# A decoder step on one core: sequence 0's keys moved beside the output projection, and the sampled rows' weight stream taken two tiles a visit

## The reference

```python
def project(x, w_in, b_f):           # q, k, v (8 heads of 64), log-sigmoid gate, u (512)
    h = einsum('bsd,dc->bsc', x, w_in)
def fox_prompt(q, k, v, logf):       # causal attention with bias F[q] - F[k], F = cumsum(logf)
def fox_sample(q, k_new, v_new, logf_new, cache_k, cache_v, cache_logf, page_table):
    k_past = cache_k[page_table]     # 32 pages of 128 positions for each sequence
    s = einsum(q, k_all) * HEAD_DIM ** -0.5 + (Fh[..., P:, None] - Fh[..., None, :])
    out = einsum(softmax(s), v_all)
def pool_mix(u_ext, ...):            # windowed means of u (2, 4, 8, 16), a 128x128 product a group
def finish(x, attn, pool, ...):
    mix = concat(attn, pool) @ w_o                         # 1024x1024
    x1 = layer_norm(ALPHA * x + mix, ln1_g, ln1_b)
    ffn = (silu(x1 @ w_gate) * (x1 @ w_up)) @ w_down       # 1024x2816, 1024x2816, 2816x1024
    return layer_norm(ALPHA * x1 + ffn, ln2_g, ln2_b)
```

## Time and profile before

| | |
|---|---|
| median of 3 runs | 1407.01 us (1405.28 to 1410.99) |
| profiled execution | 1407.72 us, span 1405.9, granted clock 0.988 |
| TensorE busy | 1350.8 us (96%), 7605 matmuls |
| VectorE, ScalarE, GpSimd busy | 693.1 (49%), 360.3 (26%), 548.9 (39%) |
| DMA | 255.56 MB, mean 182 GB/s |

### The profile page before, as it was taken

One profiled execution on the slowest core, in us unless ns is written; L12 is line 12 of the kernel. 1 busy time (PEld: TensorE's weight loads), 2 busy tenths in 40 slices (PEclk: granted clock), 3 DMA queues, 4 the chain that ended last, 5 costly groups with the idle time before them and its releaser, 6 DMA issues.

```text
span 1405.9 us, 21277 instructions
## 1 busy us (share of the span) xinstructions
PE 1350.8 (96%) x7605; PEld 1077.6 (77%) x7605; DVE 693.1 (49%) x1033; ACT 360.3 (26%) x527; POOL 548.9 (39%) x260
## 2 busy tenths in 40 slices
...
GB/s 267 95 128 136 150 162 121 151 57 38 60 109 182 92 65 228 268 239 250 221 253 225 279 245 227 245 237 264 202 271 172 182 113 183 214 265 235 230 92 120
DMA packets 111626, 255.56 MB, mean 182 GB/s; under 512 B 12832, under 2 KB 22945, under 8 KB 106136
## 3 DMA queue, kind: packets, MB, share of 16 engines
...
...
## 4 chain that ended last, share of the span: by engine, by line
PE 86%; DVE 6%; issue 2%; ACT 2%; DMA 2%; POOL 1%; SPq 1%; ACTq 0%; DVEq 0%
PE PSM L1422 32%; PE PSM L1440 16%; PE PSM L1180 10%; PE PSM L1370 6%; PE PSM L1246 4%; PE PSM L1462 4%; PE PSM L1193 3%; PE PSM L1232 3%; PE PSM L1507 2%; PE PSM L1401 1%; PE PSM L1520 1%; DMA WR<-xT 1%; PE PSM L1262 1%; DMA WR<-w_in 1%; DVE ACC L1992 1%
## 5 line engine op out<-in xcount | busy, mean ns | idle before, releaser
L815 POOL TENSOR_TENSOR WL<-WR,WH 128x1024 fp32r<-128x1024 f32 x55 | 131.9, 2399 | 431.9 <-ACT WH L1034 431.9
L755 POOL TENSOR_TENSOR AR<-AR,QB 128x1024 f32<-128x1024 f32 x96 | 231.5, 2428 | 104.2 <-DMA AR<-cache_k 90.1
L1422 PE MATMUL PSM<-XH,WH 128*128 128x512 f32 x672 | 216.8, 404 | 0.0
L1422 PE MATMUL PSM<-XH,WL 128*128 128x512 f32 x672 | 210.7, 395 | 0.0
L1422 PE MATMUL PSM<-XL,WH 128*128 128x512 f32 x672 | 210.7, 395 | 0.0
L1963 DVE TENSOR_TENSOR ACC<-ACC,PSM 128x512 f32<-128x512 f32 x160 | 108.7, 683 | 157.6 <-PE PSM L1440 157.4
L1422 PEld LDWEIGHTS PSM<-XH,WH 128*128 128x128 f32 x672 | 121.2, 188 | 62.1 <-issue 37.3
L1034 ACT CAST WH<-WR 128x1024 fp32r<-128x1024 f32 x55 | 57.5, 1047 | 366.3 <-PE PSM L1422 193.5
L1440 PE MATMUL PSM<-R 128*128 128x512 f32 x528 | 150.8, 394 | 0.0
L1422 PEld LDWEIGHTS PSM<-XH,WL 128*128 128x128 f32 x672 | 126.3, 188 | 29.9
L1422 PEld LDWEIGHTS PSM<-XL,WH 128*128 128x128 f32 x672 | 126.2, 188 | 29.6
...
## 6 DMA issues: line engine op xcount, KB each, us to landing
AR<-cache_v SPq DMA_DIRECT2D x256, 256.0 KB, 3.4
AR<-cache_k SPq DMA_DIRECT2D x192, 256.0 KB, 3.5
AR<-ws SPq DMA_DIRECT2D x37, 1024.0 KB, 4.9
...
ACC<-cache_k SPq DMA_DIRECT2D x32, 256.0 KB, 2.9
WR<-cache_k SPq DMA_DIRECT2D x32, 256.0 KB, 3.1
WR<-w_o SPq DMA_DIRECT2D x5, 1024.0 KB, 5.0
```

Of the source, the lines that this page charges most:

```text
L755: pool.tensor_tensor(keys, keys, QB[:].rearrange("p (o n) -> p o n", o=1).to_broadcast([P, KP, AW]), ALU.mult).then_inc(k_mul, 1)
L815: pool.tensor_tensor(lo, WR[:, raw_weight(e), :], hi.bitcast(F32), ALU.subtract).then_inc(ffn_lo, 1)
L1422: ins = pe.matmul(out[:, hc], (hi, lo)[a][:, k * P:(k + 1) * P], x[b][:, k, hc], start=(k == 0 and n == 0), stop=(k == KC - 1 and n == 2))
```

## The change

1. `sample_queries`, the early pieces, their ring, their DRAM scores and the waits for them are removed. The rows' query part is stored from SN to q_d by GpSimd, beside k_s and v_s.
2. Sequence 0's 16 pieces are multiplied by GpSimd ahead of the FFN's first two rests, and reduced by VectorE behind outputs 8 to 22 (KRED0). SP loads them between the weights of the output projection.
3. The FFN loop has 112 pieces: sequence 1's at units 2 to 37 (2.33 apart), the rest at 38 to 334 (3.08 apart). `queries` is gone; QB is loaded in place with a wait for k_mul.
4. The stream's tiles share units in pairs: SUNIT is 402, 402, 406, 406, 422, 422 and so on to 499, 499, 504, 37 tiles in 19 visits; SUMS move from 431, 444, 459, 473, 488, 498 to 428, 441, 456, 471, 486, 496.
5. The ring of the raw w_in tiles has three slots throughout, and tiles that shared SC, PR and PDN have places of their own or others.

```diff
+KRED0 = {8: (0,), 9: (1, 2), 10: (3,)} | {n: (n - 7,) for n in range(11, 23)}
-LATE = NB * NKP - EARLY
-KMUL = tuple(2 + ((NB - 1) * WIN - 18) * n // (LATE - 1) for n in range(LATE))
+LATE = (NB - 1) * NKP
+KMUL = tuple(2 + 35 * n // (NKP - 1) for n in range(NKP))
+KMUL += tuple(38 + ((NB - 2) * WIN - 4) * n // (LATE - NKP) for n in range(1, LATE - NKP + 1))
 KRED = tuple(u + 3 for u in KMUL)
-Q_LOAD = tuple(KMUL[NKP * n + NKP - 1] + 1 for n in range(NB - NE))
+Q_LOAD = tuple(KMUL[NKP * n + NKP - 1] + 1 for n in range(NB - 1))
-ESLOTS = [x for x in range(8, 48) if x % STEPS not in (0, 1, 11, 12, 13)]
-EMUL = tuple(ESLOTS[n * len(ESLOTS) // EARLY] for n in range(EARLY))
-ERED = tuple(x + 1 for x in EMUL)
...
-    units = {step: TSTART + SPAN_S * n // (len(order) - 1) + 3 * (n >= parts("GU", 0)) for n, step in enumerate(order)}
+    units = {step: TSTART + SPAN_S * (n // 2) // (len(order) // 2) + 3 * (n >= parts("GU", 0)) for n, step in enumerate(order)}
...
-SUNIT = {("W", n, 0): MIX + 2 * n for n in range(4)} | STEPS_S
+SUNIT = {("W", n, 0): MIX + 4 * (n // 2) for n in range(4)} | STEPS_S
...
             sp.wait_ge(ob_full, O["pv", SLOTS - 1] + 1)
+            keys(0)
+            keys(1)
             output_load_raw(2)
...
-            queries(NE)
+            sp.dma_start(QB[:], q_d[0:1, :].to_broadcast([P, AW])).then_inc(qb_ld, 16)
             sp.wait_ge(lnew_done, 1)
+            keys(2)
             output_load_raw(3)
...
+            for n in range(3, 6):
+                keys(n)
             output_load_raw(4)
-            for n in range(KS):
-                keys(n)
             sp.wait_ge(misc_st, 16 * 4)
             weight_tile(0)
+            for n in range(6, 11):
+                keys(n)
             sp.wait_ge(o_free, HRT * OC)
             pages(0, VR, 0, t["cache_v"], v_ld)
             pages(1, VR, 1, t["cache_v"], v_ld)
+            for n in range(11, NKP):
+                keys(n)
+            sp.wait_ge(k_mul, NKP)
+            sp.dma_start(QB[:], q_d[1:2, :].to_broadcast([P, AW])).then_inc(qb_ld, 16)
+            for n in range(NKP, NKP + KS):
+                keys(n)
             sp.wait_ge(wo_lo, OC + 1)
             weight_tile(1)
             weight_tile(2)
...
+            for n in range(NKP):
+                multiply(n)
             for e in range(2):
                 rest(e)
...
-            def sample_queries(m):
-                ...
-                if x in (3, 5):
-                    sample_queries((x - 3) // 2)
...
                 if n - 1 in TURN:
                     rows_lo(TURN[n - 1])
+                for c in KRED0.get(n, ()):
+                    reduce_keys(c)
                 if n == OINDEX[RT - 1, 3]:
                     output_lo(4)
```

More of the change, by code:

```diff
@@ L51 @@
 KS = 3
-KE = 4
-NE = 2
-EARLY = NE * NKP
 POOL_PAGES = 320
@@ L489, in entry @@
                 if e >= WS:
-                    before = max(n for n in range(e) if raw_slot(n) == raw_slot(e))
-                    sp.wait_ge(ent_lo, before + 1)
+                    sp.wait_ge(ent_lo, e - WS + 1)
                 if e == 1 or e > KC:
@@ L694, in _ @@
                         pages(n, VR, n % 2, t["cache_v"], v_ld, v_used, n - 1)
-                for n in range(NE + 1, NB):
-                    if u == Q_LOAD[n - NE - 1]:
-                        queries(n)
-                if o == SUBTRACT + 2 and b + 1 < NE:
-                    sp.wait_ge(m_sub, 2 * b + 2)
-                    sp.dma_start(sc, SC_d[b + 1]).then_inc(sc_ld, 16)
+                for n in range(2, NB):
+                    if u == Q_LOAD[n - 2]:
+                        sp.wait_ge(k_mul, n * NKP)
+                        sp.dma_start(QB[:], q_d[n:n + 1, :].to_broadcast([P, AW])).then_inc(qb_ld, 16)
                 if o == G_LOAD and b + 2 < NB:
@@ L724, in _ @@
             link = Chain(pool, pool_chain)
-            for tile, value in ((ones, 1.0), (PN, 0.0)):
+            for tile, value in ((ones, 1.0), (PN, 0.0), (PND, 0.0), (PD, 1.0)):
                 pool.memset(tile[:], value).then_inc(consts, 1)
@@ L777, in _ @@
                         entry_rest(n)
-                for n in range(EARLY):
-                    if EMUL[n] == x:
-                        multiply(n)
             pool.wait_ge(kn_st, 16 * PAIRS)
@@ L1704, in _ @@
                     key_lo(p, 1, 1)
-                for n in range(EARLY):
-                    if ERED[n] == x and EMUL.index(EMUL[n]) == n:
-                        reduce_keys(n)
-                if x in (3, 5):
-                    m = (x - 3) // 2
-                    dve.wait_ge(ob_full, O["q", m] + 1)
-                    dve.tensor_copy(QB[0:NB, 2 * m * P:(2 * m + 2) * P], OB[0:NB, 0:2 * P]).then_inc(ob_free, 1)
                 if x == 2:
```

207 lines of the change are left out of this document (55 added, 152 removed).

## The result

The changed kernel takes 1466.16 us in the median of six runs (1457.45 to 1470.70), the kernel before 1409.61 (1405.28 to 1411.91): a ratio of 1.0405, 95% interval 1.0378 to 1.0432. It is slower by 57 us where 7 were forecast, and far outside the range. The profiled execution took 1457.45 with a span of 1455.7; it was the fastest of the six, 8.7 under their median.

What follows compares the result with a forecast made beforehand. TensorE, busy 96 per cent of the span, was taken as the bound. Terms -7.2 - 1 + 17 + 2 + 4 + 1 - 8.7 = +7.1 gave 1414.8 against the profiled execution, 1414.1 against the median; forecast 1414.5, range 1401 to 1424.

Steps and rivals of the forecast that it cites:

- Attention loop, -8.2: Attention loop: two query products leave TensorE's chain, -7.2 us, and fewer multiplies and reduces there, -1.
- Output projection, +17 and +2 of clock: Output projection: late piece 11 and VectorE's reduces delay TensorE, +17 us (+10 to +19); half clock after the wait, +2.
- three such meetings are 2 of the 17, at that row's size: Output projection: VectorE slowed beside a multiplying GpSimd, 0.74 us lost in the row L1804, three times.
- near +22: Output projection: the term if each meeting cost up to a full multiply, as estimated from the skill page.
- Loop head, +4: FFN loop, units 0 to 44: more pieces loaded by SP ahead of two value chunks, +4 us (0 to +10).
- the forecast's 3 to 8: FFN loop's first window: sign that TensorE's waits for cache_v would sum to 3 to 8 us.
- Rest of the loop, +1: FFN loop behind its head: pieces 3.08 units apart for 3.50, value chunks mostly inside their margin, +1 us (-2 to +5).
- The QB load, nothing: FFN loop: the QB load waits for k_mul but stands one unit behind that multiply, no cost.
- Stream, -8.7: Tail, stream of sampled rows: 18 merged pairs -6.6 us, a stall missed at unit 472 -3.0, a sum at 441 +0.9.
- Rival C: FFN loop: SP saturates, second chunks of V pairs late, +20 us where the forecast had +5, 1429.8; chance 0.13.
- cache_v waits recur in every window: FFN loop: the sign by which the rival that SP saturates would hold.
- Rivals A and B: Output projection: A, reduces hidden, stall 3, 1398.8, chance 0.17; B, only VectorE's own work counts, stall 11, 1407.8, chance 0.20.

Runs made afterwards that it cites:

- skip_as_before: The changed kernel without sequence 1's 16 pieces, the other 96 at the units they had in the kernel before: ratio 1.0078 to the kernel before.
- values_by_act: The changed kernel with the FFN loop's value loads, page reads too, on ScalarE's queue: 1425.52 us, ratio 1.0104 to the kernel before.

## Why the prediction was wrong

- **Attention loop, -8.2.** Right: -6.8 in the profiled execution. Over all kernels, output 0 starts between 393.3 and 397.6 in the thirteen without the query products and between 400.1 and 402.3 in the three with them, so the term is nearer -5.5 on the average of executions.
- **Output projection, +17 and +2 of clock.** The mechanism was right at every step: piece 11 behind the values, VectorE's wait, TensorE's turn of row tile 0 at 476.0 (forecast 477.4 to 479.4). That the instant fits is in part luck. The stage had begun 6.8 earlier, which the sum had booked apart and the instants had not, so nearly the same instant is a loss of 23.6. The term that was mis-sized is "three such meetings are 2 of the 17, at that row's size". It measured 6.3 to 7.2 in outputs 8 to 20 and, with the products ready sooner, up to 10.6 over the stage. The row showed 0.74 lost, and that L1804 had started 0.94 ahead of the end of GpSimd's instruction (487.83 to 490.21); L1690 lost 1.82 at 445.30, and a rest L1514 and an L1521 near 410 to 416 some 2.2 each. The Trainium skill's rule (SBUF — State Buffer, section "Who interferes with whom"), the loser of the shared pair is blocked whole, agrees with these rows, and the estimate by it, near +22, was the better sum. It too counted three meetings: six instructions met a multiply, and lost 8.1 in all (29.9 less 21.8), 1.3 each.
- **Loop head, +4.** 9.4, inside the term's own ends. That these pieces are the cause was right: skip_as_before has the old number and 87.7. TensorE's two waits for values come to 7.7, in the forecast's 3 to 8. But the term rested on "two more pieces are multiplied than before", and the tables KMUL give 18 in units 0 to 44 for 13: five more, 11.3 us more of GpSimd in units 0 to 50 (64.94 for 53.68), not 4.9. The path is not shown to be SP's order alone, as values_by_act left the head as it was.
- **Rest of the loop, +1.** This is the step that failed: "the spacing goes from 3.50 to 3.08 units a piece; V chunks land in 3.4, mostly inside their margin: +1". It measured +31.7. I had compared a landing with the margin of the schedule before, and taken the margin as fixed. But the margin is what SP's queue leaves, and the queue was near full: the prediction counted the page reads only ahead of the first values, where they showed. A window of 50 units has 16.2 pieces in place of 14.3, some 4 pages more; at 1.07 a page that is 4 of 80 us more on SP. With the 32 pages of values, an estimate from that pace is 65 us of SP's time a window before and 69 now, ahead of the weights and of any wait; and its waits for reduces and rests, which stand in the same order, can turn one lateness into the next. The forecast also gave the loop no clock, while matmuls that ran longer are 10.1 of the 31.7.
- **The QB load, nothing.** As a wait for k_mul it costs nothing, as said: SP's waits in units 0 to 400 have no row for it. As an issue in SP's order it was worth 21 us, in the case shown behind eight value issues.
- **Stream, -8.7.** Right: -8.5, and -7.2 with nothing else changed.
- **Rivals.** Rival C was the nearest: SP is the limit in the loop. It had named +20, and 41 came; 0.13 was too little for a mechanism whose first instance stood in the earlier trace rows. Its sign, "cache_v waits recur in every window", came only in part: behind the head there are such waits in four of seven windows, 8.8 us in all, and the larger part, the 13.7 behind VectorE by way of the late query, it had not named. Rivals A and B fell: VectorE waited for the product, and the turn came at 476. The forecast treated C as a tail of a sum whose other terms were well known.
